# One block for norm, logits and routing beside the output product, and a weight ring laid over the trunk's memory

## The reference

```python
x += MemoryCrossAttention(RMSNorm(x), RMSNorm(mem))      # its last product: o @ wo
t = RMSNorm(x)                                           # norm_ffn gain
g_sel  = argmax(t @ w_group + b_group)                   # 4 groups
top_p, top_i = top_k(softmax(e_logits[rows, g_sel]), 2)  # 8 experts in the group
# each token goes to two experts: silu(xb @ w1[e]) * (xb @ w3[e]) @ w2[e], D_EXPERT = 512
out = x + sum of the two weighted expert outputs; then RMSNorm
```

## Time and profile before

| | |
|---|---|
| median of three runs | 1382.13 us |
| the profiled execution | 1379.14 us, span of its instructions 1377.2 us |
| busy share of the span | TensorE 88%, its weight loads 58%, VectorE 39%, ScalarE 30%, GpSimd 7% |
| mean granted TensorE clock | 0.97 |
| HBM traffic | 290.21 MB read, 12.93 MB written |

### The profile page before, as it was taken

The page is one execution under the profiler, slowest core; times in us unless marked ns, Lnnn a source line. Parts: engine busy times, 40 slices in busy tenths (PEclk is TensorE's granted clock), DMA queues, the critical chain, the costliest instruction groups (busy, mean ns, idle before and its releaser), DMA issues. The chain is left out here.

```text
span 1377.2 us, 15337 instructions
## 1 busy us (share of the span) xinstructions
PE 1207.4 (88%) x6038; PEld 796.1 (58%) x6038; DVE 533.0 (39%) x950; ACT 407.4 (30%) x674; POOL 92.7 (7%) x122
## 2 busy tenths in 40 slices
PE   6999999999999999999998863999777898787881
PEld 5887877777688788888886542333233333333330
DVE  4334454667757268645365535101000101000014
ACT  6234443345533442243153221112111211111112
POOL 2000000000000000000000003111111111111100
PEclk9999999999999999999999986999999999999996
DMA  7323213212123222433322059999999999999995
GB/s 272 109 72 106 79 61 112 72 62 84 46 70 104 80 92 92 154 101 102 119 96 88 1 214 356 299 412 412 411 410 413 406 403 410 415 415 413 406 404 203
DMA packets 49595, 295.25 MB, mean 214 GB/s; under 512 B 8774, under 2 KB 9174, under 8 KB 20212
## 3 DMA queue, kind: packets, MB, share of 16 engines
q1 hardware_dynamic: 40916, 274.77, 51.6%
q0 software_dynamic: 8080, 17.41, 3.8%
q10 hardware_dynamic: 528, 2.10, 0.4%
HBM read 290.21 MB, written 12.93 MB: 220 GB/s over the span
## 5 line engine op out<-in xcount | busy, mean ns | idle before, releaser
L1823 PE MATMUL e_u<-w_raw,xT 128*64 128x512 f32 x1056 | 244.6, 609 | 61.7 <-DMA w_raw<-in_w 58.4
L1823 PEld LDWEIGHTS e_u<-w_raw,xT 128*64 128x64 f32 x1056 | 82.1, 139 | 219.9 <-issue 216.3
L2147 DVE SCALAR_TENSOR_TENSOR tn<-tn,e_u 64x512 f32<-64x512 f32 x33 | 22.4, 679 | 437.9 <-ACT tn L2056 437.9
L301 DVE TENSOR_TENSOR s_lo<-s_raw,s_hi 128x2048 fp32r<-128x2048 f32 (+1 forms) x68 | 138.5, 2037 | 55.3 <-ACT s_hi L296 54.7
L296 ACT CAST s_hi<-s_raw 128x2048 fp32r<-128x2048 f32 (+1 forms) x68 | 115.9, 1704 | 110.4 <-PE pz L552 41.1
L1833 PE MATMUL e_y<-w_raw,hidT 128*64 128x512 f32 x528 | 120.6, 598 | 15.3 <-ACT hidT L2051 15.3
L520 PE MATMUL pz<-hT_hi,s_hi 128*128 128x512 f32 x288 | 116.4, 404 | 0.0
L2046 ACT COPY xT<-e_x 128x512 f32<-128x512 f32 x33 | 19.3, 585 | 321.1 <-PE e_x L1808 321.1
L520 PE MATMUL pz<-hT_hi,s_lo 128*128 128x512 f32 x288 | 112.8, 392 | 0.0
L520 PE MATMUL pz<-hT_lo,s_hi 128*128 128x512 f32 x288 | 112.6, 391 | 0.0
L536 PE MATMUL pz<-hT_hi,s_hi 128*128 128x512 f32 x256 | 102.2, 399 | 0.5
(11 more groups left out here) (366 smaller groups left out, 1860.0 us busy)
## 6 DMA issues: line engine op xcount, KB each, us to landing
w_raw<-in_w SPq DMA_DIRECT2D x192, 1024.0 KB, 28.2
s_raw<-in_w_mix SPq DMA_DIRECT2D x30, 1024.0 KB, 4.9
s_raw<-in_w_gb SPq DMA_DIRECT2D x32, 768.0 KB, 4.3
s_raw<-in_w_out_pieces SPq DMA_DIRECT2D x4, 1024.0 KB, 4.8
w_raw<-ys_scratch SPq DMA_DIRECT2D x8, 512.0 KB, 7.0
x_sb<-in_x SPq DMA_DIRECT2D x4, 512.0 KB, 4.8
rel_bias<-in_rel_tiles POOLq DMA_DIRECT2D x8, 256.0 KB, 3.0
decay<-in_decay POOLq DMA_DIRECT2D x8, 256.0 KB, 4.4
```

Source lines behind the costliest of these rows:

```text
L301: nc.vector.tensor_tensor(w_lo[n % 2][:, 0:w], w_raw[n % 2][:, 0:w], w_hi[n % 2][:, 0:w].bitcast(F32), ALU.subtract).then_inc(w_split, 1)
L1823: m = nc.tensor.matmul(ps_u[o][lo:lo + FIRST, :], xT[b][:, k * FIRST:(k + 1) * FIRST], raw[j][:, kk * FF:(kk + 1) * FF], start=k == 0, sto ...
L2147: nc.vector.scalar_tensor_tensor(tn[:], tn[:], 1.0, ps_u[b][0:FIRST, :], ALU.add, ALU.mult).then_inc(s_hm, 1)
```

## The change

The second and third block go away. Norm, turning, logits and routing are written into the mix block, tile by tile, between and behind the eight groups of the last product. The 18 slots of the ring are laid over memory that the mix block uses (`hT_hi`, `hT_lo`, the raw, high and low weight buffers, `zT`, and `vtok`), and SP loads each slot as its old content falls out of use, so that the loads begin inside the mix block.

```diff
+        PLACES = [10, 11, 0, 1, 2, 3, 12, 13, 14, 15, 4, 5, 6, 7, 8, 9, 16, 17]
+        ring_at, beyond = hT_at, hT_at + DEPTH * PW * 4
...
+            def place_free(eng, place):
+                if place < 4:
+                    eng.wait_ge(z_mm, 2 * (MIX_PIECES + Q1) + 2)
+                elif place < 6:
+                    eng.wait_ge(w_split, PIECES_ALL)
+                elif place < 10 or place == 16:
+                    eng.wait_ge(e_mm, 2 * T)
+                elif place < 12:
+                    eng.wait_ge(o_mm, T * OUT_PIECES)
+                elif place < 14:
+                    eng.wait_ge(z_mm, 2 * (MIX_PIECES + V1) + 2)
+                elif place < 16:
+                    eng.wait_ge(e_o, MX_HEADS)
+                else:
+                    eng.wait_ge(r_tb, T)
+                    for b in range(2):
+                        eng.wait_ge(s_xw[b], 16 * T // 2)
...                                      # SP, behind its last load of the mix block
+                for j in range(DEPTH):
+                    place_free(sp, PLACES[j])
+                    load_piece(sp, *ORDER[j], ORDER[j][0])
...                                      # GpSimd, in the mix block
+                pool.wait_ge(mm_tp, KD)
+                pool.wait_ge(g_lo, KD)
+                ...                      # list fill, ffn_gain, w_rt, rc, asg: loads of the constants
+                pool.wait_ge(e_o, MX_HEADS)
+                ...                      # memset of xs
+                pool.wait_ge(r_idx, 1)
+                for b in range(2):
+                    pool.wait_ge(s_xw[b], 16 * T // 2)
+                for q in range(2):
+                    pool.indirect_dma_start(xs[q][:], None, xn_dram, ...)
...                                      # TensorE
+                def rows_turned_3(t):
+                    pe.wait_ge(x2_xn, T + t + 1)
+                    wait_over(pe, r_ea, t)
+                    wait_over(pe, r_ed, t)
+                    for k in range(KD):
+                        last = nc.tensor.transpose(pa[4 + k // 4][:, k % 4 * P:(k % 4 + 1) * P], xn3[t % 2][:, k::KD],
+                                                   ident[:])
+                def logits(t):
+                    pe.wait_ge(r_ea, t + 1)
+                    pe.wait_ge(r_ed, t + 1)
+                    for k in range(KD):
+                        last = nc.tensor.matmul(pz[0][:, t * LOGITS:(t + 1) * LOGITS], h3T[t % 2][:, k, :], w_rt[:, k, :],
+                                                start=(k == 0), stop=(k == KD - 1))
...                                      # inside the loop over the groups g
+                    if g == 3:
+                        rows_turned_3(0)
+                    if g == 5:
+                        rows_turned_3(1)
+                        logits(0)
+                rows_turned_3(2)
+                logits(1)
+                logits(2)
+                rows_turned_3(3)
+                logits(3)
...                                      # ScalarE
+                for t in range(T):
+                    act.wait_ge(e_x, 2 * t + 2)
+                    nc.scalar.activation(squared[:], x_sb[:, t, :], ACT.Square, accum_out=sums3[:, t:t + 1])
+                    act.wait_ge(x2_ms, T + t + 1)
+                    nc.scalar.activation(sums3[:, t:t + 1], sums3[:, t:t + 1], ACT.Sqrt)
+                    if t:
+                        h3_in(t - 1)
+                    act.wait_ge(x2_xn, T + t + 1)
+                    act.dma_start(xn_dram[t * P:(t + 1) * P, :], xn3[t % 2][:]).then_inc(s_xw[t % 2], 16)
+                h3_in(T - 1)
...                                      # VectorE
+                for t in range(T):
+                    for half in range(2):
+                        ...              # the add of group 2t + half to x_sb
+                    if t:
+                        h3_in(t - 1)
+                    ...                  # mean, reciprocal
+                    if t > 1:
+                        dve.wait_ge(r_tb, t - 1)
+                        dve.wait_ge(s_xw[t % 2], 16)
+                    nc.vector.scalar_tensor_tensor(xn3[t % 2][:], x_sb[:, t, :], sums3[:, t:t + 1], ffn_gain[:],
+                                                   ALU.mult, ALU.mult).then_inc(x2_xn, 1)
...                                      # the experts' block
-                for piece in ORDER[EARLY_SLOTS:DEPTH]:
-                    load_piece(sp, *piece, piece[0])
-                fetch(0)
-                fetch(1)
```

More of the change, by code:

```diff
@@ new lines, in trunk, with load_piece, __init__, __call__ @@
+        AT.update({piece: OVER_AT + PIECES + i for i, piece in enumerate(SECOND_HALF)})
+        ORDER = sorted(AT, key=AT.get)
+        def load_piece(sp, q, n, e):
+            j = AT[q, n] % DEPTH
+            src, h = (w13v[n % 2], n // 2) if n < 4 else (w2v, n - 4)
+            sp.dma_start(raw[j][:], src[bass.ds(e, 1), :, h * PW:(h + 1) * PW].rearrange("o p f -> p (o f)")
+                         ).then_inc(s_raw[j], 16)
+        class Area:
+            def __init__(self, at, size):
+                self.at, self.end = at, at + size
+            def __call__(self, name, shape, dt=F32):
+                size = 4
+                for n in shape[1:]:
+                    size *= n
+                got = nc.alloc_sbuf_tensor_at(name, shape, dt, offset=self.at)
+                self.at += -(-size // 32) * 32
+                assert self.at <= self.end, (name, self.at, self.end)
+                return got
@@ new lines, in trunk @@
+        w_rt = table_area("w_rt", [P, KD, LOGITS])
+        fill = table_area("fill", [P, EXPERTS * LIST // P], I32)
+        iota = rc[:, 2 * P:2 * P + EXPERTS]
+        r0 = 2 * P + EXPERTS
+        slot_no = rc[:, r0:r0 + P]
+        r0 += P
+        blk_thr, blk_at, blk_e = (rc[:, r0 + JOB_BLOCKS * i:r0 + JOB_BLOCKS * (i + 1)] for i in range(3))
+        r0 += 3 * JOB_BLOCKS
+        rank1, half_no = rc[:, r0:r0 + 1], rc[:, r0 + 1:r0 + 2]
+        at_slot = work_area("at_slot", [P, 2 * T, P], F32R)
@@ L380, in trunk @@
                 sem("m_" + n) for n in ("s", "mx", "exp", "nrm", "t", "pT", "o", "ohi", "olo", "mm", "x"))
+            r_c, r_ta, r_tb, r_ea, r_ed, r_lg, r_fl, r_fw, r_gm, r_ex, r_hot, r_pc, r_at, r_it, r_idx = (
+                sem("r_" + n) for n in ("in", "turned_a", "turned_b", "h3_act", "h3_dve", "logits", "filled", "list",
+                                        "gmax", "gexp", "hot", "places", "at_slot", "ids", "idx"))
+            s_xw = [sem(f"xn_stored{b}") for b in range(2)]
             s_ident, s_small, s_rows = (sem("in_" + n) for n in ("ident", "small", "rows"))
@@ L1747, in trunk @@
             ys_halves = ys_dram.rearrange("s (h d) -> (s h) d", h=2)
[L1750 removed]
+            s_ys = [sem(f"e_ys{b}") for b in range(2)]
+            s_used = [sem(f"e_used{j}") for j in range(DEPTH)]
+            s_scattered = sem("scattered")
             s_tx, s_xT, s_tn, s_h3, s_hm, s_hd, s_ht, s_hT, s_yo = (
```

449 lines of the change are left out of this document (164 added, 285 removed).

## The result

| | median | executions |
|---|---|---|
| kernel before, beside it | 1381.95 us | 4, 1381.66 to 1382.44 |
| changed kernel | 1357.82 us | 4, 1357.47 to 1358.68 |

The ratio is 0.9826, 95% interval 0.9809 to 0.9843: 24.1 us or 1.7% less. The forecast was 1356.8. The profiled execution took 1358.68 us (span 1356.9), 20.5 us less than the profiled one of before. So the traces have 20.5 us to explain, not 24.1.

The account below looks back on a forecast made before the run. The DMA stream of the experts' pieces bounds the kernel, so its restart counts: 19th piece at 850.3 instead of 876.59 us, 26.3 less 1.0 for scatters, gives 1382.1 - 25.3 = 1356.8 us; range 1352 to 1368.

Parts of the forecast that it names:

- the rule of the sum: Experts' stage: the kernel ends as much earlier as SP issues the 19th piece earlier, 25.3 us after deductions.
- Loads inside the mix block: First twelve pieces land before 797 us under work needing no DMA; cost nothing, and no gain by themselves.
- The insertions: Turning and logits put between the last product's groups: logits reach VectorE at 817.9 instead of 832.48 us, 14.6 us earlier.
- The border: Between mix and experts' blocks: gathers issued, then 1.5 us of semaphore clearing; jobs write at 846.3 us, 11.2 us earlier.
- The landing of the jobs write: On SP's queue with no piece ahead: 4.0 us instead of 19.1, bounds 2.6 to 19.1, so 15.1 us earlier.
- The slot: First ring slot freed by half of the first up products at 849.1 us, just in time for the 19th piece.
- Scatters: List scatters beside the restarted stream: most fall where it is idle, last issued at 848 us; 1.0 us of slowed start.
- A: Rival: jobs write stays late, behind scatters and gathers; 1372 us with the full 19.1 us, between 1363 to 1372; chance 0.14.
- B: Rival: stores starve, so VectorE scales tile 2 at 813 instead of 803 us, 10 us late; 1367 us; chance 0.05.
- C: Rival: stream's rate falls with the ring at other addresses; at 0.2 us more a piece 1391 us, slower; chance 0.03.
- D: Rival: no change, since the end is not bound by the restart; 1382 us; chance 0.02.
- E: Rival: write and gather land at lower bounds, scatters cost nothing; gain 28 to 30 us, 1353 us; chance 0.06.

Follow-up runs that it names:

- before_free4: Kernel before, with SP's wait for the jobs write moved behind four more ring pieces (19th to 22nd): 1379.63 us, ratio 0.9983 to the kernel before.
- scatters_late: Changed kernel with the eight list scatters moved from the start of the experts' block to the fifth job: 1359.55 us, ratio 0.9841 to the kernel before.
- loads_at_end: Changed kernel with all 18 first ring loads held until the last product ends: 1365.40 us, ratio 0.9883 to the kernel before.
- pool_early: Changed kernel with the first two gathers and GpSimd's waits for index and stores moved out of the mix block: 1351.22 us, ratio 0.9783 to before.
- hold_ring: Changed kernel with SP holding the 19th piece until the second expert's last up product frees its piece: 1365.33 us, ratio 0.9879 to the kernel before.
- turns_late: Changed kernel with tiles 0 and 1 turned and tile 0's logits made behind the last product, not within it: 1364.55 us, ratio 0.9876 to before.

## Why the prediction was right, and which of its steps were not

**The bound, and the rule of the sum.** The stream as the bound holds (389 to 420 GB/s in the slices of the stage, the last landing followed by the same 41 us). The rule that the kernel ends as much earlier as the 19th piece is issued earlier **failed as a cause**: `before_free4` issued it 10 us earlier for 1 to 3 us. What accounts for the runs better is the work of the DMA engines. In the kernel before they are kept busy from 849.38 us, when SP issues the last six pieces. SP's timeline of the kernel before:

```profile
849.38 3.06 SPq L1520 DMA_DIRECT2D w_raw<-in_w  x6
```

From there 180 pieces at 2.624 us are 472.3, the scatters 10.8, the gap in front of the restart 2.9 us, together 1335.4; the last piece landed at 1336.27. In the changed kernel they are kept busy from 852.41 with 174 pieces, 456.6 us, and 6.9 more, which I put down to what is left of the scatters and to the gathers. This 6.9 is a remainder (463.5 - 456.6), not a measurement of its own. The difference of the traces, 20.3 us, splits like this:

| | us |
|---|---|
| six pieces no longer in the busy stretch, 6 x 2.624 | 15.7 |
| scatters mostly in the idle stretch, 10.8 - 6.9 (remainder) | 3.9 |
| the gap in front of the restart gone | 2.9 |
| the busy stretch starts later, 852.41 instead of 849.38 | -3.0 |
| sum | 19.5 |

With the second traces of both kernels (gap 4.6, surplus 4.9, start 853.75 instead of 848.98) the same terms give 21.4 for 22.4 measured. The close fit leans on the 10.8 us of the one slow trace of `scatters_late`: with the 7.1 us that its median gives, the kernel before would end its loads at 1331.7, 4.6 us early. With the 10.8 us, the terms give for `before_free4` 850.6 + 472.3 + 10.8 = 1333.7, and 1338.3 was measured: 4.6 us of low rate at full share stay unexplained (1.8 of them may be chance, since that execution took 1381.42 us against a median of 1379.63). The restart rule hit the number nearly, because in the kernel before the jobs write landed just when the six pieces and the scatters had been worked off, so that both readings count nearly the same stretch, 26.5 us of work and 27.2 from 849.38 to 876.59.

**Loads inside the mix block: right.** 12 pieces moved under the work, 292 to 429 GB/s from 755 to 775 and again from 785. Priced at nothing there, and rightly; by `loads_at_end` the early start is worth 9 us, which the sum did not have as a term of its own.

**The insertions: nearly right.** Logits at full clock take 1.87 us (2.0 forecast). But the last turning took 1.95 instead of 1.07 and the last logits 3.60 instead of 2.0, as the granted clock fell to 0.82 from 810 and 0.50 from 815 us; the logits came at 820.23 instead of 817.9. The product itself began 0.8 us later. **Routing: right,** 15.6 us to the start of `idy`; the gather at 837.11 instead of 834.4 inherits the delay.

**The border: wrong by 4.6 us.** Forecast: gathers issued, then 1.5 us. Measured: 8.6 us between `idy` and the next block, most of it GpSimd's DRAIN of 5 us. `pool_early` takes 6.6 us of the border away. VectorE started at 844.72 instead of 838.2, and the jobs write went out at 851.32 instead of 846.3.

**The landing of the jobs write: wrong the other way.** At most 1.1 us instead of 4.0, and below the lower bound of 2.6, which was the landing of 512 KB and so no bound for 128 bytes. The 2.0 us of the Trainium skill ("DMA: Bandwidth & Descriptors", "Anatomy of one DMA — SWDGE (gpsimd) path") were too many too. The page fits them to transfers that GpSimd issues; SP issued this one, so its rule was stretched in the prediction. The two errors nearly cancelled: 19th piece at 852.41, 850.3 forecast. **The slot:** it comes free at about the time at which the write has landed, as forecast, and is what SP waited for last, 0.8 us. But that was at 852.4 instead of 849.1 us: the gather landed after 2.9 us, not 7.9, and its rows then lay waiting for the border, to be turned at 844.87.

**Scatters: mis-sized.** 1.0 us forecast; 4.9 to 6.9 are left over in the two traces. The last one went out at 854.84, not 848, and so beside the restarted stream.

So 25.3 us were forecast on the axis of the traces and 20.3 measured; the median came out within 1 us because the two profiled executions lie on opposite sides of their medians. By the second traces it is 22.4, by medians 24.1 and 25.1, so some 3 us of the gain by medians are in no trace and are assigned to nothing. The size of the hit is partly luck, the sign and the main mechanism are not.

**The rivals.** A (write stays late) is out: 1.1 us. B is out: stores of 512 KB land after 2.8 us in the median, and tile 2 is scaled at 803.15 us; only the fourth store, which nothing but the 18th piece and GpSimd waited for, took longer, 7.9 us. C is out: 2.624 us a piece in `hold_ring`, against 2.64 before. D is out as stated; yet `before_free4` shows that half of it was true of the kernel before: an earlier restart by itself did not move its end. E was nearest on the landings of write and gather (still too high on both) and missed the scatters.

**Open:** why the DRAIN takes 5.05 us behind gathers that land in 2.8, and 2.4 without them; the 4.6 us of `before_free4`; and the chain from VectorE's first step to the jobs write, which took 6.6 us in the changed kernel but 8.1 in `pool_early` and before. Of these 1.5 us, 1.2 lie in one step: a TENSOR_SCALAR to `act_b` takes 1.50 us in `pool_early` and before, where GpSimd's MEMSET of `xo` runs at the same time, and 0.29 in the changed kernel, where that MEMSET is over. Why it does is not shown.

## What to carry to other kernels

When a stream of transfers is the bound, count the work that its engines still have from the moment they are kept busy, small scattered items included; a wait on the issuing queue that ends late costs little as long as the engines are busy behind it (here 1 to 3 us for 10.8). Move work out of that stretch (whole pieces, scatters) rather than moving waits. And before work is put at the end of a block, look at what has to leave the engine before all engines meet: a gather issued 5 us earlier was paid back with 3.5 us more of border for everybody, and GpSimd's last waits in the block with 3 more.

## What the runs showed of the hardware

- Eight scatters of 128 items of 4 bytes each take 7 to 11 us of stream time, as much as 3 to 4 pieces of 1 MB (`scatters_late` against `hold_ring`). With the engines otherwise idle each lands 2.1 us after its issue (`hold_ring`), on the full stream after 7.8 (`scatters_late`), in the median.
- Two transfers of 128 and some 300 bytes to HBM have landed at most 1.1 us after the second one's issue when no piece is ahead of them, and 19.1 behind 6 MB and the scatters.
- GpSimd's DRAIN at the end of a block took 5.05 us with two indirect gathers just issued and 2.43 with the waits for them alone. TensorE's took 4.13 us behind two added products and 0.57 without them.
- TensorE's granted clock was 1.00 up to 810 us (busy 5.00 of 5 us), 0.82 from 810 to 815 (busy 4.74) and 0.50, the lower of its two levels, from 815 (busy 4.07); 16 products of 36 columns then took 3.60 us instead of 1.87. In `turns_late` the clock stayed at 0.50 from 810 to 820 us although TensorE was busy all 10 us.
